# Three norms applied after their projections, and the expert down products with the expert rows as moving operand

## The reference, cut to what matters

```python
for layer in range(2):                        # first block, h is [256, 1024]
    xn = rmsnorm(h, norm_mix[layer])
    h = h + (attn_retention_mixer if layer == 0 else short_conv_mixer)(xn, ...)
    h = h + peer(rmsnorm(h, norm_ffn[layer]), ...)
return rmsnorm(h, final_norm)
# short_conv_mixer: bg, cg, hx = split(xn @ w_in, 3); u = cg * hx
#                   y = causal convolution of width 3 of u;  return (bg * y) @ w_out
# peer, per token: hid = gelu(xn @ u[chosen].T); out = (gate * hid) @ v[chosen]
# rmsnorm(x, g) = x * rsqrt(mean(x * x) + EPS) * g,  EPS = 1e-6
# second block: 16 meta tokens are put ahead, then
h = h + 0.5 * swiglu(rms_norm(h, ffn1_norm), w_in, w_out)   # silu(gate) * up, D_FF = 2816
```

## Time and profile before

| what | value |
|---|---|
| time, median of 3 runs (lowest to highest) | 2663.62 us (2663.00 to 2664.08) |
| time of the profiled execution | 2662.47 us |
| span of the profiled execution | 2660.7 us |
| mean granted TensorE clock | 0.986 of full |
| TensorE / weight loads busy | 97% / 95% |
| VectorE / ScalarE / GpSimd busy | 73% / 45% / 4% |
| DMA | 429.55 MB, 161 GB/s |

### The profile page before, as it was taken

The page is one execution under the profiler, slowest core; times in us unless marked ns, Lnnn a source line. Parts: engine busy times, 40 slices in busy tenths (PEclk is TensorE's granted clock), DMA queues, the critical chain, the costliest instruction groups (busy, mean ns, idle before and its releaser), DMA issues.

```text
span 2660.7 us, 57759 instructions
## 1 busy us (share of the span) xinstructions
PE 2577.1 (97%) x21894; PEld 2517.3 (95%) x21894; DVE 1944.2 (73%) x3972; ACT 1184.0 (45%) x1738; POOL 107.6 (4%) x64
## 2 busy tenths in 40 slices
PE   8899999999999999999999999999999998999999
PEld 7789999999999999999999999999999998778999
DVE  6679986667886787789966668966876547666663
ACT  4455554444444434455544443544334334444442
POOL 0024000000000000051000000000000000000000
PEclk9999999999999999999999999999999998999999
DMA  5334445555345554544355554355544453623454
GB/s 214 113 127 154 148 142 182 183 188 183 135 141 189 182 186 160 185 151 166 111 183 188 182 190 166 107 186 190 182 150 151 173 169 134 137 97 136 165 183 151
DMA packets 120708, 429.55 MB, mean 161 GB/s; under 512 B 14690, under 2 KB 16738, under 8 KB 120176
## 3 DMA queue, kind: packets, MB, share of 16 engines
q1 hardware_dynamic: 118464, 420.65, 45.6%
q0 software_dynamic: 2096, 6.93, 1.4%
HBM read 423.79 MB, written 3.74 MB: 161 GB/s over the span
## 4 chain that ended last, share of the span: by engine, by line
PE 87%; DVE 8%; ACT 2%; DMA 2%; issue 1%; DVEq 0%; ACTq 0%
PE work L440 16%; PE work L441 16%; PE work L442 16%; PE acc L440 10%; PE acc L441 10%; PE acc L442 10%; PE work L739 5%; DVE ring_lo L434 2%; DMA ring<-in_gate_in 2%; PE work L545 1%; PE work L904 1%; DVE arena L1707 1%; DVE rstd L1291 1%; ACT ring_hi L428 0%; PE work L876 0%
## 5 line engine op out<-in xcount | busy, mean ns | idle before, releaser
L434 DVE TENSOR_TENSOR ring_lo<-ring,ring_hi 128x1024 fp32r<-128x1024 f32 (+1 forms) x759 | 921.2, 1217 | 497.1 <-ACT ring_hi L428 495.0
L428 ACT ACTIVATE ring_hi<-ring 128x1024 fp32r<-128x1024 f32 (+1 forms) x799 | 830.8, 1051 | 503.4 <-PE acc L442 383.2
L440 PE MATMUL work<-normed_hi,ring_hi 128*128 128x256 f32 (+1 forms) x3344 | 961.0, 287 | 33.5 <-DVE normed_lo L1301 19.8
L441 PE MATMUL work<-normed_lo,ring_hi 128*128 128x256 f32 (+1 forms) x3344 | 951.4, 285 | 0.0
L442 PE MATMUL work<-normed_hi,ring_lo 128*128 128x256 f32 (+1 forms) x3344 | 944.0, 282 | 0.0
L440 PEld LDWEIGHTS work<-normed_hi,ring_hi 128*128 128x128 f32 x3344 | 639.6, 191 | 39.8 <-issue 22.1
L441 PEld LDWEIGHTS work<-normed_lo,ring_hi 128*128 128x128 f32 x3344 | 635.4, 190 | 0.6
L442 PEld LDWEIGHTS work<-normed_hi,ring_lo 128*128 128x128 f32 x3344 | 635.6, 190 | 0.0
L441 PE MATMUL acc<-weighed,ring_hi 128*128 128x256 f32 x2048 | 575.5, 281 | 0.0
L440 PE MATMUL acc<-weighed,ring_hi 128*128 128x256 f32 x2048 | 575.1, 281 | 0.0
L442 PE MATMUL acc<-weighed,ring_lo 128*128 128x256 f32 x2048 | 574.9, 281 | 0.0
(11 more groups left out here) (216 smaller groups left out, 2431.2 us busy)
## 6 DMA issues: line engine op xcount, KB each, us to landing
ring<-in_u SPq DMA_DIRECT2D x256, 512.0 KB, 3.2
ring<-in_v SPq DMA_DIRECT2D x256, 512.0 KB, 3.2
ring<-in_ffn_in SPq DMA_DIRECT2D x88, 512.0 KB, 3.2
ring<-in_query SPq DMA_DIRECT2D x32, 512.0 KB, 3.2
ring<-in_ffn_out SPq DMA_DIRECT2D x32, 512.0 KB, 4.5
ring<-in_even_in SPq DMA_DIRECT2D x28, 512.0 KB, 4.2
ring<-in_odd_in SPq DMA_DIRECT2D x24, 512.0 KB, 3.2
ring<-in_mix_in SPq DMA_DIRECT2D x19, 512.0 KB, 3.2
```

The costliest lines, as they stand in the source:

```text
L428: act.activation(ring_hi[:, n % RING, 0:width], ring[:, n % RING, 0:width], ACT.Copy).then_inc(hi_ready, 1)
L434: eng.tensor_tensor(ring_lo[:, n % RING, 0:width], ring[:, n % RING, 0:width], ring_hi[:, n % RING, 0:width].bitcast(F32), ALU.subtract).t ...
L440: pe.matmul(out, w_hi, hi, start=start, stop=False, **more)
L441: pe.matmul(out, w_hi, lo, start=False, stop=False, **more)
```

## The change: what it does

1. `down` takes 128 tokens of `weighed` as the stationary operand and 512 columns of v's block as the moving one: 12 matmuls of 512 columns a chunk. `acc` then holds tokens by features.
2. At the end of `peer`, ScalarE and VectorE copy `acc` to SBUF (`by_token`), TensorE transposes it back into `acc` (16 transposes), and the additions into the stream follow.
3. Norms 2, 4 and 5 are gone as stages. `lead_norm` makes the parts of stream times gain at once (for `ffn1`: the product of the two gains), block by block with the additions. The squares are summed by one VectorE `tensor_reduce`; one matmul on TensorE (`mean_square`) ahead of the fourth projection gives the mean. Norms 4 and 5 become one factor: squares are taken with scale sqrt(gain4^2 + EPS), the root with bias EPS^2.
4. In `odd` the factor enters as its square on `cg` and once on `y_tmp`. In `ffn1` VectorE multiplies gate and up results by it as it reads them from PSUM, and ScalarE's Silu comes after that from SBUF.
5. Norm 4's result is written into the stream during `ffn1` (a second sum, root and reciprocal, then one product per block at c = 14 to 21). The meta tokens' parts are made in `peer(1)`.

```diff
@@ TensorE, peer @@
                 def down(n, e, i=0, slots=4):
-                    for k in range(K):
-                        mm = product3(pe, acc[:, k // 2, (k % 2) * S:(k % 2 + 1) * S], n, k, weighed[:, 0, e % 4, :], weighed[:, 1, e % 4, :],
-                                      e == 0 and k % 2 == 0, e == CHUNKS - 1, skip_group_check=True)
+                    m = n % RING
+                    for t in range(NT):
+                        by_hi, by_lo = [weighed[:, x, e % 4, t * P:(t + 1) * P] for x in range(2)]
+                        for x, (tokens, rows) in enumerate(((by_hi, ring_hi), (by_hi, ring_lo), (by_lo, ring_hi))):
+                            for half in range(2):
+                                mm = pe.matmul(acc[:, 2 * half + t, :], tokens, rows[:, m, half * 512:(half + 1) * 512], ...)
...
+                for c in range(K):
+                    pe.wait_ge(first_turned, 2 * l + c // 4 + 1)
+                    pe.wait_ge(second_turned, 2 * l + c // 4 + 1)
+                    for t in range(NT):
+                        mm = pe.transpose(acc[:, c // 2, (c % 2) * S + t * P:(c % 2) * S + (t + 1) * P], by_token[:, t, c * P:(c + 1) * P], ident)
+                    mm.then_inc(back_done, 1)
+            def mean_square(bank, width, count):
+                pe.wait_ge(sum_ready, count)
+                pe.matmul(acc[:, bank, 0:width], cst("inv_d"), square_sum[:, 0:width], start=True, stop=True).then_inc(sum_done, 1)
@@ TensorE, odd (feed_forward(1) likewise, and mean_square(1, S, 3) at i == 24) @@
-                project_two(W0["odd"], SLOT0["odd"], XS, 2)
+                project_two(W0["odd"], SLOT0["odd"], XS, lead_lo, 0)
                 for i in range(2, len(ODD_ITEMS)):
+                    if i == 3:
+                        mean_square(0, S, 1)
                     project(W0["odd"] + i, SLOT0["odd"] + i, XS)
@@ ScalarE @@
+                act.wait_ge(chunk_used, (l + 1) * CHUNKS)
+                for half in range(2):
+                    act.activation(by_token[:, 0, half * 512:(half + 1) * 512], acc[:, 2 * half, :], ACT.Copy).then_inc(first_turned, 1)
+                lead_norm(l)
+            def lead_norm(l):
+                for k in range(K):
+                    act.wait_ge(stream_block, l * K + k + 1)
+                    act.activation(normed_hi[:, k, XS], stream[:, k, XS], ACT.Copy, scale=gain).then_inc(lead_hi, 1)
+                    act.activation(squares[:, k, XS], stream[:, k, XS], ACT.Square, ...).then_inc(lead_square, 1)
+                    if k == 4:
+                        split_to(n)
...
+                split_to(n + 1)
+                act.wait_ge(sum_done, l + 1)
+                act.activation(rstd[...], acc[:, 0, ...], ACT.Sqrt, ...).then_inc(root_ready, 1)
@@ VectorE @@
-                for k in range(K):
-                    dve.tensor_tensor(stream[:, k, XS], stream[:, k, XS], acc[...], ALU.add).then_inc(stream_block, 1)
+                for half in range(2):
+                    dve.tensor_copy(by_token[:, 1, half * 512:(half + 1) * 512], acc[:, 2 * half + 1, :]).then_inc(second_turned, 1)
+                lead_norm(l)
+            def lead_norm(l):
+                for k in range(K + 1):
+                    if k < K:
+                        dve.wait_ge(back_done, l * K + 2 * (k // 2) + 2)
+                        dve.tensor_tensor(stream[:, k, XS], stream[:, k, XS], acc[...], ALU.add).then_inc(stream_block, 1)
+                    if k:
+                        dve.wait_ge(lead_hi, l * K + k)
+                        dve.scalar_tensor_tensor(normed_lo[:, k - 1, XS], stream[:, k - 1, XS], gain, normed_hi[...], ALU.mult, ALU.subtract).then_inc(lead_lo, 1)
+                split_to(n)
+                dve.wait_ge(lead_square, K + l * (K + 1))
+                dve.tensor_reduce(square_sum[:, 0:width], squares[:, :, TA - width:TA].rearrange("p k t -> p t k"), AX.X, ALU.add).then_inc(sum_ready, 1)
+                split_to(n + 1)
+                dve.wait_ge(root_ready, l + 1)
+                dve.reciprocal(rstd[:, 0:width], rstd[:, 0:width]).then_inc(vec.sem, vec.up())
+                step()
+                if l == 0:
+                    dve.tensor_tensor(spare, rstd[:, 0:S], rstd[:, 0:S], ALU.mult).then_inc(vec.sem, vec.up())
@@ VectorE, odd, each group @@
+                        dve.tensor_tensor(cg[:, b, :], cg[:, b, :], spare, ALU.mult)
...
+                        dve.tensor_tensor(y_tmp[:, b, 0, :], y_tmp[:, b, 0, :], rstd[:, 0:S], ALU.mult)
@@ VectorE, feed_forward(1), each c @@
+                        dve.tensor_tensor(ff_gate[:, c % 2, :], work[:, w % 4, 0:width], rstd[:, 0:width], ALU.mult)
...
+                        dve.tensor_tensor(ff_hid[:, c % 2, :], work[:, w % 4, 0:width], rstd[:, 0:width], ALU.mult)
+                        dve.wait_ge(silu_ready, c + 1)
+                        dve.tensor_tensor(ff_hid[:, c % 2, :], ff_hid[:, c % 2, :], ff_silu[:, c % 2, :], ALU.mult)
@@ the stages, on all three engines @@
-            norm(2, XS)
             odd()
...
-            norm(4, XS)
-            norm(5, ALL)
             feed_forward(1, ALL)
```

More of the change, by code:

```diff
@@ L555, in project, with project_two @@
                 mm.then_inc(bank_done[w % 4], 1)
[L557 removed]
+            def project_two(w, n, cols, ready, count):
                 width = cols.stop - cols.start
@@ L1538, in peer @@
                 split_to(SLOT0[f"query{l}"])
-                norm(2 * l + 1, XS, None, lambda k: k == 3 and split_to(SLOT0[f"query{l}"] + 1))
+                norm(2 * l + 1, XS, lambda k: k == 3 and split_to(SLOT0[f"query{l}"] + 1))
                 split_to(SLOT0[f"query{l}"] + 2)
+                if l:
+                    dve.wait_ge(meta_in, 16)
+                    scaled = product[:, 0, 0:K * META].rearrange("p (k t) -> p k t", k=K)
+                    dve.tensor_tensor(scaled, stream[:, :, 0:META], gains[:, 5, :].unsqueeze(2).to_broadcast([P, K, META]), ALU.mult).then_inc(meta_scaled, 1)
+                    dve.wait_ge(meta_scaled, 2)
+                    dve.tensor_tensor(normed_lo[:, :, 0:META], scaled, normed_hi[:, :, 0:META].bitcast(F32), ALU.subtract).then_inc(vec.sem, vec.up())
                 choose(l)
@@ L1669, in feed_forward @@
                     split_to(SLOT0[f"ffn{x}"] + i)
-                    if kind == "ffup":
-                        w = W0[f"ffn{x}"] + i
+                    w = W0[f"ffn{x}"] + i
+                    if kind == "ffgate" and x == 1:
+                        dve.wait_ge(*done(w))
+                        dve.tensor_tensor(ff_gate[:, c % 2, :], work[:, w % 4, 0:width], rstd[:, 0:width], ALU.mult).then_inc(bank_free[w % 4], 1)
+                        if c == 9:
+                            dve.wait_ge(square4_ready, K)
+                            dve.tensor_reduce(square_sum[:, 0:S], squares4[:, :, :].rearrange("p k t -> p t k"), AX.X, ALU.add).then_inc(sum_ready, 1)
+                        elif c == 13:
+                            dve.wait_ge(root_ready, 3)
+                            dve.reciprocal(spare, spare).then_inc(vec.sem, vec.up())
+                            step()
+                        elif c > 13:
+                            k = c - 14
+                            dve.scalar_tensor_tensor(stream[:, k, XS], stream[:, k, XS], gains[:, 4, k:k + 1], spare, ALU.mult, ALU.mult).then_inc(vec.sem, vec.up())
+                    elif kind == "ffup" and x == 1:
+                        dve.wait_ge(*done(w))
+                        dve.tensor_tensor(ff_hid[:, c % 2, :], work[:, w % 4, 0:width], rstd[:, 0:width], ALU.mult).then_inc(bank_free[w % 4], 1)
+                        dve.wait_ge(*freed(w))
+                        dve.wait_ge(silu_ready, c + 1)
+                        dve.tensor_tensor(ff_hid[:, c % 2, :], ff_hid[:, c % 2, :], ff_silu[:, c % 2, :], ALU.mult).then_inc(vec.sem, vec.up())
+                        step()
+                        parts(c, cols, ff_hid[:, c % 2, :], ff_ready, ff_hi, ff_lo)
+                    elif kind == "ffup":
                         dve.wait_ge(*freed(w - 1))
@@ L1771, in _ @@
             peer(1)
-            norm(4, XS, stream)
-            dve.wait_ge(meta_in, 16)
-            norm(5, ALL)
             feed_forward(1, ALL)
```

122 lines of the change are left out of this document (86 added, 36 removed).

## The result

The changed kernel takes 2645.57 us (median of 4 runs, 2641.84 to 2651.07) beside 2663.85 for the kernel before on the same chip: ratio 0.9933, 95% interval 0.9916 to 0.9951, so 18.3 us less where 48.3 had been forecast. The profiled execution is the slowest of the four (2651.07, span 2649.3), so spans are compared stretch by stretch. "Surplus" is, as in the prediction, what a product takes beyond one column a cycle at 2.4 GHz (106.7 ns at 256 columns, 213.3 at 512).

A forecast was written before the change was run, and what follows sets the result against it. TensorE's pace was taken to bound the expert loops, with standstills at the norms between stages. Down products -36.3 us and norms -12.0 sum to -48.3: 2614.2 from the profiled 2662.47, 2615.3 as median; range 2586 to 2646.

The forecast's parts named there:

- Down products: Expert loops: 512-column matmuls at 225.0 ns, a chunk 2700 ns instead of 2842, 36.3 us less over 256 chunks.
- rival B: Down products: surplus goes with columns, 233.6 ns by slope and 2641 us, or 2652 in full proportion; chance 0.23.
- A: The forecast itself, down products: surplus belongs to the instruction, 11.7 ns at either width, time 2615; chance 0.55.
- The prediction's 2644: Kernel's time by the Trainium skill's N / 2.4 + 2.5 ns: down products save 30 ns a chunk, 7.7 us.
- The removed norms: Ends of peer(0) and peer(1): 2.7 and 12.7 us less; with the small terms, norms together -12.0 us.
- the stall ahead of item 4: In odd and ffn1: new TensorE stalls of 3.7 and 2.7 us, VectorE's split standing behind the root.
- `tensor_reduce`: New norms on VectorE: 1.04 ns an element, 2.3 us for 2048 elements, 2.45 us for 2176 in ffn1.
- Small terms: Third `mean_square` in ffn1 0.44 us, meta parts in peer(1) about 0.6, one clock excursion 2.4, all added.
- VectorE and loads: Expert loops: VectorE's 2.54 us round fits into 2.70, loads rise from 185 to 195 GB/s, no wait expected.
- D: Down products: fp32r reading from the ring can't feed 512 columns without pauses; at 245 ns, 2677 us; chance 0.05.
- E: New norms: the waits behind the root eat what the norms give, time 2627 us; chance 0.05.
- C: Down products: surplus, from loads and matmuls nearly equal in length, goes at double length; 217 ns, 2590 us; chance 0.12.

The follow-up runs named there:

- e5: Kernel before with the new down products alone, copies and transposes included, norms as they were: 2652.77 us, ratio 0.9956.
- e2: Changed kernel with each 512-column down product cut into two of 256, operands in the same roles, 24 to a chunk: 2653.05 us, ratio 0.9967.
- m1: Rows of 97 equal products in an otherwise idle kernel, both operands at the same place within 256 bytes: 119.9 ns at 256 columns, 226.7 at 512.
- e7: Kernel before with the new down products alone, plus 32 unused bytes that bring `weighed` to place 0: 2636.97 us, ratio 0.9900.
- e4: Kernel before with only an unused tensor of 64 bytes a partition added, moving everything allocated behind it: 2647.50 us, ratio 0.9950.
- e1: Changed kernel with the old 256-column down products, so without copies and transposes, norms as changed: 2639.65 us, ratio 0.9911.
- e6: Changed kernel plus an unused tensor of 224 bytes a partition that brings `weighed` to the same place as v's rows: 2627.02 us, ratio 0.9867.
- m3: Products alone, one thing changed a row: at 512 columns 226.7 ns with other banks or order, 233.5 with the moving operand 2 elements on.
- m4: Map of products alone, both operands at every 16th of 128 elements: at 512 columns 227.3 ns at equal places, others up to 233.6.

## Why the prediction was wrong

The sign was right, and 2645.57 lies just inside the range (2586 to 2646); the size was wrong: 18.3 us of 48.3.

**Down products: the step that failed.** "I take 225.0: 256 chunks x 142 ns = 36.3 us less." The pace was 233.3, a chunk 2800 ns, 10.3 us less than at 118.3; e5, with the copies and transposes, gained 10.9. 26 of the missing 30 us are here. The step carried the surplus of a 256-column product over to a 512-column one unchanged. At the places that the change gives its operands it is 11.7 ns at 256 columns (e2) and 20.0 at 512, so there the surplus is not by the instruction, and the figure is that of rival B (233.6 ns, 2641). B's reason does not hold in general either: at equal places the surplus is 13.2 to 13.4 ns at 256, 320, 384 and 512 columns, and inside the kernel a product of 512 columns takes 226.7 once 224 unused bytes are put ahead of `weighed`. So A's mechanism holds at equal places, and even there at 13.4 ns: 225.0 was reached in no run. Missing from the list of bounds was the place of the operands, which moves the pace by 6.6 ns at 512 columns and from 113.3 to 120.0 at 256. It also made and the earlier trace rows poor evidence: 118.4, 117.8 and 125.0 were products at different places, and the slope of 7.2 ns for 16 columns that kept B alive compared places as much as widths; at one place, in m1, it is 5.5 (119.9 to 125.3). With the place put right the change gives 36 us of the 48, and the down products by themselves 26.8 of the 36.3 (before to e7, by their starts). The prediction's 2644, from a surplus of 2.5 ns at either width, comes near the measured time by accident: no fp32r row has that surplus.

**The removed norms.** Forecast -12.0. Three pairs of kernels, each the same down products without and with the new norms, give -10 (e4 to e1), -10 (e7 to e6) and -7 (e5 to the change, whose intervals overlap). First projections, the stall ahead of item 4 in both places and its cause came as written (3.7 and 2.7 us forecast, 3.47 and 2.42 idle). Item 4 came at 21.5 and 21.5 us after the last product where 20.1 and 19.4 were written, so the two ends gave 1.3 and 10.6 instead of 2.7 and 12.7. The mis-sized term is `tensor_reduce`: 2.3 us from a slope of 1.04 ns an element, 3.69 measured, 1.80 ns an element; 3.93 instead of 2.45 in ffn1. The new one reads its eight elements 1088 bytes apart; that this makes it dearer wasn't tried. The trace of the kernel before had a nearer row than the one that was used: L1531 makes eight sums over a strided view of 128 elements in 412 ns, where L1359 makes one sum of 128 in 286.

```profile
L1531 DVE TENSOR_REDUCE arena<-arena 128x8 f32<-128x128 f32 x4 | 1.6, 412 | 0.1
L1359 DVE TENSOR_REDUCE small<-arena 128x1 f32<-128x128 f32 x4 | 1.1, 286 | 0.1
```

Whether the stride or the number of sums costs more is open. The Trainium skill (SBUF — State Buffer, Door 1: The DMA port swizzle) says that accesses that cross to a new 16-byte line pay a penalty, which would point that way; no run here tells it apart.

**Small terms.** The clock fell twice, not once more: 19% of 9 us and 17% of 10 us are 3.4 us lost, where 2.4 were charged. With these the sum is -10.3 - 1.3 - 10.6 + 0.4 + 0.6 + 3.4 = -17.8; measured -18.3. The longer measures of the two ends bear the norms' terms out: 0.4 us more and 8.4 less, with the clock's share and the third `mean_square` in them. That the two meet so closely is partly luck: the interval is -13 to -22, and the profiled execution that the terms are read from is only 11.4 us shorter than the one before. It loses about 5 us to the clock in a stage that the change doesn't touch: 0.86 over 2280 to 2330, where e1, with the same code there, has 0.97.

```profile
2280.00:2330.00 50.00, 48.56 (x260) 35.57 (x259) 26.56 (x65) 19.89 (x56) 3.56 (x4) 0.86 0.55 137
```

The 0.4 and 0.6 weren't tried by themselves.

**VectorE and loads.** VectorE didn't bound, as forecast, but at 2800 ns a chunk that was a mild test; e6 ran at 12 x 226.7 = 2720 and held its pace too. That refutes D, whose pause in reading the ring would show there; E falls with the pairs, two of them clear of noise, and C with the map, whose fastest wide product took 226.7.

**What stays open.** Why 256 bytes are the period, why equal places suit wide products and hurt narrow ones, and why narrow products at one pair of places settle at more than one pace: the old order at place 8 (116.7 in the kernel, 117.9 alone), the `odd` projections (116.7 before, 117.8 in e4), and m3 against m4 (113.4, 117.7). The products that ran before them differ in each case; no run changes that alone.

## What to carry over

Before a matmul pace is put down to width, count or traffic, look at where its two operands lie within 256 bytes: an unused tensor of the right size is the cheapest experiment there is, and here it was worth as much as the rewrite of the loop. When a change adds even a small tensor, everything allocated behind it moves, so compare it with a kernel that has the same addresses, and read one tile's pace in both, over all stages and not in one stretch alone. A reduction over a strided view is priced from one of the same stride and number of sums, and what stands on VectorE behind the wait for its result is written down before the wait is added.

## What the runs showed of the hardware that was not expected

fp32r products of one shape, at full clock, take 113.3 to 120.1 ns at 256 columns and 226.7 to 234.2 at 512 when only the places of their operands change. At 512 columns the place within 256 bytes settles the pace to about 1 ns; at 256 it doesn't, and the same places gave 113.4 and 117.7. At equal places the first five gaps of a wide chunk that comes after up products were 228 to 236 ns, before they settled at 227 (e6, e7). 64 unused bytes made the kernel before 14.5 us (0.5%) faster, 32 made it 6 us slower. ScalarE, VectorE and 148 GB/s of loads beside the products cost them nothing. At 448 columns, at equal places, a product took 206.6 ns, a surplus of 19.9 where 384 and 512 had 13.4.
